# ScalarE instead of GpSimd multiplies attention's probabilities by the reciprocal of their sum

## The reference

```
for window, dilation in ((128, 1), (512, 4), (2048, 16)):
    m = max(scores);  p = exp(scores - m);  l = sum(p);  o = (p @ v) / l
out = sum(w * o) / sum(w)        # w = l * exp(m - max of the three m)
```

## Time and profile before

| | us |
|---|---|
| median of 3 runs | 2446.87 |
| the runs | 2445.83 to 2446.91 |
| the profiled execution: its own time | 2446.62 |
| its span, from the first to the last instruction | 2444.8 |
| attention's norms run (start) | 794.5 to 1161.0 |
| `k_hi` of the four groups (start) | 784.4, 878.6, 970.2, 1060.8 |

### The profile page before, as it was taken

One profiled execution on the slowest core, in us unless ns is written; L12 is line 12 of the kernel. 1 busy time (PEld: TensorE's weight loads), 2 busy tenths in 40 slices (PEclk: granted clock), 3 DMA queues, 4 the chain that ended last, 5 costly groups with the idle time before them and its releaser, 6 DMA issues. The chain is left out here.

```text
span 2444.8 us, 29433 instructions
## 1 busy us (share of the span) xinstructions
PE 2283.6 (93%) x10358; PEld 1852.0 (76%) x10358; DVE 1783.9 (73%) x2666; ACT 844.2 (35%) x1299; POOL 271.8 (11%) x204
## 2 busy tenths in 40 slices
PE   5999999999999999999989777997699999999996
PEld 4788888888878777778778565885488888888885
DVE  7777777777688877777573577777877777777766
ACT  5322222222253655556213443223332222222222
POOL 3000000000001333323000245201300000000000
PEclk9999999999999999999999888998799999999998
DMA  3111111111431010101112323212311111111122
GB/s 145 39 52 52 51 51 51 51 52 51 137 114 52 18 35 18 35 18 36 43 43 95 122 78 105 85 44 99 116 35 52 52 51 51 51 55 60 42 101 105
DMA packets 52325, 155.60 MB, mean 64 GB/s; under 512 B 5904, under 2 KB 7952, under 8 KB 50064
## 3 DMA queue, kind: packets, MB, share of 16 engines
q1 hardware_dynamic: 52240, 154.51, 18.9%
HBM read 133.18 MB, written 21.30 MB: 63 GB/s over the span
## 5 line engine op out<-in xcount | busy, mean ns | idle before, releaser
L967 DVE TENSOR_TENSOR acc<-psum,acc 128x512 f32<-128x512 f32 x288 | 197.9, 691 | 160.9 <-PE psum L580 158.1
L578 PE MATMUL psum<-act_hi,tile_hi 128*128 128x512 f32 x704 | 277.0, 394 | 13.2 <-DVE acc L602 8.3
L579 PE MATMUL psum<-act_lo,tile_hi 128*128 128x512 f32 x704 | 275.7, 392 | 0.0
L580 PE MATMUL psum<-act_hi,tile_lo 128*128 128x512 f32 x704 | 275.5, 391 | 0.0
L682 ACT CAST t_hi<-t_raw 128x512 fp32r<-128x512 f32 x144 | 89.5, 622 | 313.7 <-DVE t_raw L823 306.3
L578 PEld LDWEIGHTS psum<-act_hi,tile_hi 128*128 128x128 f32 x704 | 133.3, 189 | 45.5 <-DVE acc L602 11.9
L580 PEld LDWEIGHTS psum<-act_hi,tile_lo 128*128 128x128 f32 x704 | 133.1, 189 | 27.9
L579 PEld LDWEIGHTS psum<-act_lo,tile_hi 128*128 128x128 f32 x704 | 133.2, 189 | 27.3
L1804 DVE TENSOR_TENSOR probs_t_lo<-psum,probs_t_hi 128x512 fp32r<-128x512 f32 x144 | 96.7, 686 | 55.3 <-ACT probs_t_hi L1730 55.3
L704 ACT ACTIVATE sum<-sum 128x512 f32<-128x512 f32 x72 | 45.6, 633 | 246.1 <-DVE sum L921 151.4
L454 PE MATMUL psum<-norm_hi,plain_hi 128*128 128x512 f32 x288 | 112.0, 389 | 0.0
(11 more groups left out here) (369 smaller groups left out, 5788.5 us busy)
## 6 DMA issues: line engine op xcount, KB each, us to landing
tile_lo_raw<-in_d SPq DMA_DIRECT2D x40, 512.0 KB, 4.3
gate_raw<-in_gu SPq DMA_DIRECT2D x36, 512.0 KB, 3.8
up_raw<-in_gu SPq DMA_DIRECT2D x72, 256.0 KB, 3.6
raw_tile<-in_w_xz SPq DMA_DIRECT2D x19, 512.0 KB, 3.6
gate_up_lo_raw<-in_gu SPq DMA_DIRECT2D x8, 1024.0 KB, 5.1
cum_rows<-cum_scratch SPq DMA_DIRECT2D x8, 1024.0 KB, 4.9
raw_tile<-in_w_out SPq DMA_DIRECT2D x16, 512.0 KB, 3.6
raw_tile<-in_w_att SPq DMA_DIRECT2D x11, 512.0 KB, 3.5
```

The costliest lines, as they stand in the source:

```text
L578: pe.matmul(o, w_h[:, s, d, :], a_h[:, s, x], start=(s == 0), stop=False)
L579: pe.matmul(o, w_h[:, s, d, :], a_l[:, s, x], start=False, stop=False)
L580: mm = pe.matmul(o, w_l[:, s, d, :], a_h[:, s, x], start=False, stop=(s == 1))
L967: v.tensor_tensor(x, banks(4 + d % 4), x, ALU.add).then_inc(sem(p + "_acc"), 1)
```

## The change

The norm is done by ScalarE: an activation of kind Copy whose scale is the column of reciprocals, in place, in ScalarE's list. The planner is told so, with a cost of 0.24 + 0.105 us a block in place of 0.34 + 0.086, and places all steps of the stretch anew by the same rules. GpSimd keeps the cosine products.

```diff
--- before.py
+++ after.py
@@ -1444,7 +1444,7 @@
                 add("DVE", "max", ("max", g, i, hh), 0.14 + 0.125 * w, ("score", g, i, hh), ("mask_in",), ("v", CH - 1))
                 add("ACT", "exp", ("exp", g, i, hh), 0.27 + 0.105 * w, ("max", g, i, hh))
                 add("DVE", "recip", ("recip", g, i, hh), 0.17, ("exp", g, i, hh))
-                add("POOL", "norm", ("norm", g, i, hh), 0.34 + 0.086 * w, ("recip", g, i, hh))
+                add("ACT", "norm", ("norm", g, i, hh), 0.24 + 0.105 * w, ("recip", g, i, hh))
             for n, (g, i, j) in enumerate(BLOCKS):
                 u = CH * g + i
                 add("PE", "turn", ("turn", g, i, j), 0.62, ("norm", g, i, 3), ("low", *BLOCKS[n - 2]) if n > 1 else None)
@@ -1723,6 +1723,12 @@
                 act.activation(pr, pr, ACT.Exp, bias=nmax[:, c:c + 1], scale=-1.0, accum_out=den[:, c:c + 1])\
                    .then_inc(sem("at_exp"), 1)
 
+            def norm(g, i, hh):
+                n, c = 32 * g + 4 * i + hh, 4 * (i % 2) + hh
+                act.wait_ge(sem("at_rden"), n + 1)
+                pr = probs(i, hh)[:, 0:(i + 1) * P]
+                act.activation(pr, pr, ACT.Copy, scale=rden[:, c:c + 1]).then_inc(sem("at_norm"), 1)
+
             def high(g, i, j):
                 n = NT * g + cnt(i, j)
                 act.wait_ge(sem("at_t_mm"), n + 1)
@@ -1736,6 +1742,8 @@
                     first_act(act, step, e)
                 elif step == "exp":
                     soft(*e)
+                elif step == "norm":
+                    norm(*e)
                 elif step == "high":
                     high(*e)
                 elif step == "end_lo":
@@ -1855,19 +1863,11 @@
                 gp.tensor_tensor(qn[:, t, x], qr[:, x], cos[:, x], ALU.mult).then_inc(sem("at_cos"), 1)
 
         def att_pool(gp):
-            def norm(g, i, hh):
-                n, c = 32 * g + 4 * i + hh, 4 * (i % 2) + hh
-                gp.wait_ge(sem("at_rden"), n + 1)
-                pr = probs(i, hh)[:, 0:(i + 1) * P]
-                gp.tensor_scalar(pr, pr, rden[:, c:c + 1], 1.0, ALU.mult, ALU.mult).then_inc(sem("at_norm"), 1)
-
             for step, *e in MIXER["POOL"]:
                 if step in TAIL_STEPS:
                     tail_pool(gp, step, e)
                 elif step == "first_cos":
                     first_pool(gp, *e)
-                elif step == "norm":
-                    norm(*e)
                 else:
                     g, t = NEXT_TILES[e[0]]
                     piece_pool(gp, g, 4 * t + e[1])
```

## The result

The changed kernel takes 2481.83 us in the median of 4 runs (2479.09 to 2485.99), the kernel before 2446.89 beside it: 34.9 us or 1.4% slower, ratio 1.0144 with a 95% interval from 1.0126 to 1.0161. The forecast was 2453.7, in a range from 2440 to 2467. The direction held, the size did not, and the time lies outside the range.

The account below looks back on a forecast made before the run. TensorE was taken to bind the groups and the transpose, cast, subtraction, product chain the tail. Terms -1.7 + 6.2 + 2.3 = +6.8 us on 2446.62 gave 2453.4, or 2453.7 as median, range 2440 to 2467.

Parts of the forecast that it names:

- What bounds the kernel now: Attention stretch: TensorE binds the four groups, the chain binds the last 15.80 us, and GpSimd is not late.
- What the step costs: 128 norms on ScalarE: 87.6 to 99.1 us, 99.1 taken, 24.8 a group; no table reload.
- Taken away: Norms leaving GpSimd: 0 to 4.1 us won at the change to group 4, 1.7 taken for `q_lo` subtractions.
- ScalarE's load: Groups 1 to 3: ScalarE 87 to 89% busy with the norms, adding 0 to 12.4 us, 6.2 taken.
- The last group: Fourth group's end: four norms may lie behind the other work, lengthening the bare tail 0 to 4.6 us, 2.3 taken.
- the first rival: Four groups: ScalarE's waits absorb the norms and the planner orders around them; 2445 to 2449 us, chance 0.26.
- Rival "much slower, the gap at each change of group": Norms block ScalarE's casts at three changes of group, TensorE runs out of fill; 19.8 us, 2467, chance 0.12.
- The slow clock: After the gap before group 4: TensorE's clock at 1.2 GHz from 1071.88 to about 1076.7, 2.4 us lost.
- What would show it: Attention: right if ScalarE is busy 80 to 88 us a group; wrong if new gaps exceed 3 us with slow clock.

Follow-up runs that it names:

- better ranks: Changed kernel, norms on ScalarE, with ScalarE and VectorE ranks chosen among 864 sets by the planner's own end; 2433.71 us, ratio 0.9937.
- the tenth: Kernel before, norms on GpSimd, with ScalarE and VectorE ranks chosen among 432 sets by the planner's own end; 2438.93 us, ratio 0.9962.
- the kernel with casts first: Changed kernel, with ScalarE's `high` casts and unit's end ranked before other steps that could start at the same moment; 2446.11 us, ratio 0.9988.

## Why the prediction was wrong, by its own steps

- *What bounds the kernel now.* Right: TensorE binds, the tail is bare, and GpSimd is not late. The sentence that the question is "what sets the end of that stretch alone" held: 34.4 of the 39.4 us between the two profiled spans lie in the stretch.
- *What the step costs.* Right, slightly high: 94.4 us against 87.6 to 99.1 and 99.1 taken. No further table load.
- *Taken away.* The term was -1.7 for the `q_lo` block. The rows of the changed kernel at the last change of group:

```profile
1092.58 4.97 DVE L1713 TENSOR_TENSOR q_hi_lo<-q_k_next,q_hi_lo 64x1024 fp32r<-64x1024 f32 x4
1097.59 0.16 DVE L1807 RECIPROCAL denom_recip<-denom 128x1 f32<-128x1 f32 x1
1097.67 0.67 DVE L1820 TENSOR_TENSOR staged_conv_in<-psum,rstd_rows 128x512 f32<-128x512 f32 x1
```

```profile
1098.39 0.80 PE L1505 MATMUL psum<-norm_hi,tile_hi 128*128 128x512 f32 x1 [6.39 <-DVE staged_conv_in L1820]
```

  The block takes 4.97 us in place of 6.60: 1.6 of the 1.7 us are there, and in all VectorE was busy 307.0 us in the stretch before and 306.2 after, so it gained little from norms that left GpSimd. But the gap behind the block has grown to 6.39 us, since the new order reaches it with less work left for TensorE: before, TensorE ran on for 3.3 us after the block's start (1064.45 to 1067.7), now it stops 0.6 us ahead of it (1092.0). The hope that a shorter block makes a shorter gap failed.
- *ScalarE's load, +6.2 (0 to 12.4).* This step failed. It took capacity, 82 of 94 us, and today's waits as the measure, and both ends of the range were built on how full the engine would be; for the new order it had no term at all, and it spoke of one only as something that could bring the cost below 0. The runs show in its place: 22 to 24 us come with the new order, with the load taken off; 11 to 13 more with the load in that order; and with better ranks the same 317 us fit into a stretch 51 us shorter. What failed as well is the sentence in the first rival that "the planner knows the new costs and orders around them". A greedy list schedule looks at nothing behind a step. It doesn't know that a cast has `low`, `values` and the next transposes hanging on it, while in the changed kernel's trace the first transposes of a unit start 4.2 us after its last norm has ended (median of the 32 units; 0.2 us at the least). Ranking the casts and the unit's end first is worth 4.6 us with norms on GpSimd and 36 with norms on ScalarE.
- *The last group, +2.3 (0 to 4.6).* The place was right, and the size far off: the tail lasts 36.7 us in place of 15.8, with 10.4 us of idle time and a granted clock of 0.86.
- *Rival "much slower, the gap at each change of group"*, 2467. Nearest to the truth in size, but it had the wrong mechanism. There are gaps at two changes of group (6.39 us, and 4.67 at 988.93), but norms that wait on their reciprocal cost 1.0 us in all, and both gaps are there in the new order with the norms on GpSimd too, so no norm that ScalarE carries out makes them. The rows of that run:

```profile
988.25 1.12 PE L1656 MATMUL psum<-ident,probs_even 128*128 128x128 f32 x4 [4.66 <-DVE probs_t_lo L1809]
...
1092.81 0.79 PE L1510 MATMUL psum<-norm_hi,tile_hi 128*128 128x512 f32 x1 [6.25 <-DVE staged_conv_in L1817]
```

- *The slow clock* was priced only as something to win, 2.4 us. It became a third of the loss: 11.8 us.
- *What would show it.* Of the signs for being right, the norms' durations held (0.39 to 1.14 us on average by width) and the tail is over 17 us. ScalarE's 80 to 88 us a group did not come (71.0 to 79.5), nor did groups longer by about 2 us each (5.9 shorter, 14.1 and 19.4 longer). One sign for being wrong came: new gaps over 3 us with the clock down behind them.

The planner's lists are written in the kernel, and their order was part of the change. The forecast treated a new plan as a small disturbance; it is the largest term of the sum.

## What to carry to other kernels

Where a list schedule sets the order, a moved step is also a new plan: ask which step now has to share its engine with the step that the critical chain hangs on, and which of the two the tie rule lets go first. How full the engine is didn't tell the loss here: ScalarE was 73% busy over the stretch in the changed kernel and 83% in the fastest one. Ranking the casts and the unit's end first was worth 36 us here and cost nothing. And if a moved step's load is suspected, take the load away while the order is kept: what stays is the order. When the ranks are changed as well, compare with a kernel before that has the same ranks.

## What the runs showed that I had not expected

- In nine of the ten kernels compared with the one before, the planner's own end gave the change of the median to within 4 us, over a span from 14 us faster to 50 slower; the tenth fell 7 us short. The planner knows no slow clock, so it got the sums right without their parts.
- TensorE's idle time brought half as much again in slow clock. From the kernel before to the changed one idle time rose by 22.6 us, and the same instructions were busy 11.8 us longer; from the changed one to the one with the better ranks on ScalarE they fell by 34.3 and 16.8. In the changed kernel the clock fell right behind a gap of 2.06 us, and in the kernel with casts first behind one of 1.51 (to 1075.15); in the kernel before, gaps of 1.68 and 1.48 us had a granted clock of 1.00 behind them, and so had one of 1.68 us in the changed kernel (to 898.24). The length of a single gap doesn't tell them apart here.
